# An eleven-stage encoder layer: the stage ends without GpSimd's drain and with one barrier instead of two; the merge's stores waited for one stage later

## The reference, cut to what matters

```python
u = _rmsnorm(h, g_mix); proj = u @ w_in                      # split into q, k, v, z, xbc, dt
att = _diff_attention(q, k, v, ...); ssm = _ssm_branch(z, xbc, dt, ...)
g_a, g_s = jnp.split(jax.nn.sigmoid(u @ w_gate + b_gate), 2, axis=-1)
merged = g_a * (att @ w_att_up) + g_s * (ssm @ w_ssm_up)
h = h + merged @ w_out
u2 = _rmsnorm(h, g_ffn)
h = h + _expert_choice(u2, w_router, w_exp_gate, w_exp_up, w_exp_down)   # 16 experts
ple_gate = jax.nn.sigmoid(h @ w_ple_gate + b_ple_gate)
h = h + ple_gate * (p @ w_ple_proj)
return _rmsnorm(h, g_final)
```

## Time and profile before

| what | value |
|---|---|
| median of 3 runs | 3064.95 us (3060.66 to 3067.93) |
| span of the profiled execution, first to last instruction | 3063.1 us |
| the profiled execution's own time | not listed apart from its span; the median is 1.9 us above the span |
| mean granted TensorE clock | 0.942 |
| busy share: TensorE, VectorE, ScalarE, GpSimd | 89%, 51%, 42%, 10% |
| DMA | 530.38 MB, mean 173 GB/s |

### The profile page before, as it was taken

How to read it: one execution, slowest core, us unless ns; L and a number is a source line. 1 busy time by engine, 2 the same in 40 slices (tenths; PEclk the granted TensorE clock), 3 DMA queues, 4 the chain that set the end, 5 groups by cost and what they waited for, 6 DMA issues and landing times. The chain is left out here.

```text
span 3063.1 us, 41071 instructions
## 1 busy us (share of the span) xinstructions
PE 2725.8 (89%) x15360; PEld 2333.1 (76%) x15360; DVE 1575.4 (51%) x2141; ACT 1291.4 (42%) x1801; POOL 313.8 (10%) x323
## 2 busy tenths in 40 slices
PE   6999999896788688596997987799999999999698
PEld 4899888685666266484885875699999999999686
DVE  5000000261776888312763227577777777777555
ACT  4111111141666754322542113355555555555445
POOL 1000000000000022211110002001101101101022
PEclk9999999898999899797998997699999999999899
DMA  5713112275320443846874644578878878878442
GB/s 181 228 69 104 69 69 77 87 243 155 79 79 22 126 134 106 264 157 219 281 257 151 205 137 167 169 230 246 262 231 246 259 234 247 259 234 246 150 156 90
DMA packets 422970, 530.38 MB, mean 173 GB/s; under 512 B 18424, under 2 KB 358280, under 8 KB 420840
## 3 DMA queue, kind: packets, MB, share of 16 engines
q1 hardware_dynamic: 391088, 396.13, 41.1%
q0 software_dynamic: 31776, 132.83, 13.4%
HBM read 400.78 MB, written 128.12 MB: 173 GB/s over the span
## 5 line engine op out<-in xcount | busy, mean ns | idle before, releaser
L2146 DVE TENSOR_TENSOR ex_w_lo<-ex_w_raw,ex_w_hi 128x2048 fp32r<-128x2048 f32 x195 | 443.9, 2291 | 142.8 <-ACT ex_w_hi L2103 142.8
L2235 PE MATMUL ex_ps_u<-ex_x,ex_w_hi 128*128 128x384 f32 x2048 | 411.6, 342 | 5.1 <-DVE ex_w_lo L2146 5.1
L2103 ACT ACTIVATE ex_w_hi<-ex_w_raw 128x2048 fp32r<-128x2048 f32 x195 | 370.5, 1909 | 0.8
L2235 PEld LDWEIGHTS ex_ps_u<-ex_x,ex_w_hi 128*128 128x128 f32 x2048 | 349.2, 189 | 6.2 <-issue 5.5
L2235 PEld LDWEIGHTS ex_ps_u<-ex_x,ex_w_lo 128*128 128x128 f32 x2048 | 265.7, 191 | 0.6
L2254 PE MATMUL ex_ps_d<-ex_w_hi,ex_h 128*128 128x512 f32 x768 | 266.0, 401 | 0.0
L2235 PE MATMUL ex_ps_u<-ex_x,ex_w_lo 128*128 128x192 f32 x2048 | 265.4, 273 | 0.0
L356 DVE TENSOR_TENSOR w_lo<-w_raw,w_hi 128x2048 fp32r<-128x2048 f32 x14 | 32.1, 2293 | 404.8 <-ACT w_hi L322 404.8
L328 ACT ACTIVATE stage<-ps 128x512 f32<-128x512 f32 (+1 forms) x102 | 55.7, 547 | 401.6 <-PE ps L380 336.7
L2254 PE MATMUL ex_ps_d<-ex_w_lo,ex_h 128*128 128x512 f32 x512 | 202.9, 396 | 0.0
L2254 PEld LDWEIGHTS ex_ps_d<-ex_w_hi,ex_h 128*128 128x128 f32 x768 | 144.7, 188 | 35.0
(11 more groups left out here) (393 smaller groups left out, 4933.0 us busy)
## 6 DMA issues: line engine op xcount, KB each, us to landing
ex_w_raw<-in_w_exp_gate SPq DMA_DIRECT2D x64, 1024.0 KB, 8.3
ex_w_raw<-in_w_exp_up SPq DMA_DIRECT2D x64, 1024.0 KB, 6.2
ex_w_raw<-in_w_exp_down SPq DMA_DIRECT2D x64, 1024.0 KB, 6.5
w_raw<-in_w_in SPq DMA_DIRECT2D x15, 1024.0 KB, 6.3
mg_w_raw<-in_w_ssm_up SPq DMA_DIRECT2D x24, 512.0 KB, 6.0
mg_g_raw<-g_d SPq DMA_DIRECT2D x24, 512.0 KB, 7.5
xbcT_d<-stage POOLq DMA_DIRECT2D x5, 1536.0 KB, 5.7
cv_raw<-xbcT_d POOLq DMA_DIRECT2D x10, 768.0 KB, 6.4
```

The source lines that it names most:

```text
L2103: act.activation(unit(w_hi, j), w_raw[:, j % RAW], ACT.Copy).then_inc(w_hi_done, 1)
L2146: dve.tensor_tensor(unit(w_lo, j), w_raw[:, j % RAW], unit(w_hi, j).bitcast(F32), ALU.subtract).then_inc(w_split, 1)
L2235: last = pe.matmul(ps_u[:, j % 2, m, 0:wide * C], w[:, s // 2, k, s % 2, cols], x[:, k, 0:wide].rearrange("p a c -> p (a c)"), start=i == ...
```

## The change

`Block()` gets `no_gpsimd_drain=True` in all eleven stages: the other four engines still drain, GpSimd does not, and all meet in one barrier of semaphores. The callback no longer clears and meets; it puts the stage's semaphores on a list, and the next stage's `open_block` has GpSimd clear that list at its start, while the other engines go on. After the last stage the list is cleared and one full `nc.all_engine_barrier()` follows, with a DRAIN on every engine, GpSimd's too. The semaphores of the merge's stores now live in `encoder_layer`; GpSimd no longer waits for the last stores at the end of `merge_branches`, SP does so in `project_out` before its loop that reads them. And SP's two increments of `m_in` come before its first loads.

```diff
@@ stage_semaphores
-    def clear():
-        nc.clear_and_free_semaphores(used)
-        nc.all_engine_barrier()
-    ctx.callback(clear)
+    ctx.callback(lambda: DONE_WITH.extend(used))
     return sem
+def open_block(nc, ctx):
+    if DONE_WITH:
+        nc.clear_and_free_semaphores(DONE_WITH)
+        DONE_WITH.clear()
+    return ctx.enter_context(nc.Block(no_gpsimd_drain=True))
@@ every stage
-        block = ctx.enter_context(nc.Block())
+        block = open_block(nc, ctx)
@@ merge_branches (its out_done is now the argument out_done)
-        out_done = [sem("out0"), sem("out1")]
...
-            for done in out_done:
-                pool.wait_ge(done, 32 * NU // 2)
             pool.wait_ge(next_in, 16 * 4)
@@ project_out, SP
             w_view = w_out.rearrange("(k p) (c n) -> c p k n", p=P, n=BLK)
+            for s in range(2):
+                sp.sem_inc(m_in[s], 32)
             for c, ks in enumerate(PARTS):
                 sp.dma_start(w_raw[:, ks], w_view[1, :, ks]).then_inc(w_in[c], 16)
...
             for s in range(2):
-                sp.sem_inc(m_in[s], 32)
                 sp.dma_start(xt[:, s], x[s]).then_inc(x_in[s], 16)
+            for done in m_stored:
+                sp.wait_ge(done, 32 * KT * NB // 2)
             with sp.Fori(0, TT // 2 - 1) as it:
@@ encoder_layer
+        m_stored = [nc.alloc_semaphore("m_stored%d" % s) for s in range(2)]
...
+        DONE_WITH.extend(m_stored)
...
             embed_and_norm(nc, tiles(h), tiles(ple), wg_hi, wg_lo0, w_ple_gate, b_ple_gate, g_final, ident, y_tiles)
+    nc.clear_and_free_semaphores(DONE_WITH)
+    DONE_WITH.clear()
+    nc.all_engine_barrier()
```

More of the change, by code:

```diff
@@ L43 @@
 START = 1
+DONE_WITH = []
 class Chain:
@@ L1442, in _, with merge_branches @@
                 sp.wait_ge(g_out[s], 16 * (NG // 2))
-def merge_branches(nc, g_d, o_hi_d, o_lo_d, yT_d, var_d, g_ssm_norm, w_att_up, w_ssm_up, b_gate, m_hi_d, m_lo_d, o_hi, o_lo, y_hi, y_lo, y_raw, w_out):
+def merge_branches(nc, g_d, o_hi_d, o_lo_d, yT_d, var_d, g_ssm_norm, w_att_up, w_ssm_up, b_gate, m_hi_d, m_lo_d, o_hi, o_lo, y_hi, y_lo, y_raw, w_out, out_done):
     KO = VW // P
@@ L1661, in _, with project_out @@
                 last.then_inc(full, 1)
-def project_out(nc, m_hi_d, m_lo_d, x, w_out, w_raw, m_slots, w_hi, w_lo, g_ffn, w_router, ident, logits, h_d, u2_d):
+def project_out(nc, m_hi_d, m_lo_d, x, w_out, w_raw, m_slots, w_hi, w_lo, g_ffn, w_router, ident, logits, h_d, u2_d, m_stored):
     HB = D // BLK
@@ L2482, in encoder_layer @@
             half_raw = keep("half_raw", [P, KT, BLK], F32)
-            merge_branches(nc, g, o_hi, o_lo, yT, var, g_ssm_norm, w_att_up, w_ssm_up, b_gate, m_hi, m_lo, *turned, *halves, half_raw, w_out)
-            project_out(nc, m_hi, m_lo, x, w_out, half_raw, turned[1], *halves, g_ffn, w_router, ident, logits, tiles(h), tiles(u2))
+            merge_branches(nc, g, o_hi, o_lo, yT, var, g_ssm_norm, w_att_up, w_ssm_up, b_gate, m_hi, m_lo, *turned, *halves, half_raw, w_out, m_stored)
+            project_out(nc, m_hi, m_lo, x, w_out, half_raw, turned[1], *halves, g_ffn, w_router, ident, logits, tiles(h), tiles(u2), m_stored)
+        DONE_WITH.extend(m_stored)
         with nc.sbuf_tensor("wg_hi", [P, KT, D], F32R) as wg_hi, nc.sbuf_tensor("wg_lo0", [P, KT, BLK], F32R) as wg_lo0:
```

## The result

| | before | changed |
|---|---|---|
| median of 4 runs each | 3063.44 us | 3045.79 us |
| range | 3060.66 to 3067.93 | 3041.91 to 3048.51 |
| ratio (95% interval) | | 0.9941 (0.9927 to 0.9955) |
| span of the profiled execution | 3063.1 us | 3046.9 us |

The change makes the kernel 17.7 us faster by the medians, 0.6%. The median of before, with one more run, is now 3063.44.

A forecast was written before the change was run, and what follows sets the result against it. TensorE, busy 2725.8 of 3063.1 us, bounds the kernel untouched; only time around the eleven stage ends can go. 7.8 + 4.4 + 7.0 + 1.9 = 21.1 us gained, 8.7 paid, 12.4 net: 3052.5 us, range 3042 to 3063.

The forecast's parts named there:

- The likeliest case: Whole kernel: 21.1 us gained, 8.7 paid at the last drain, 12.4 us faster, 3052.5 us; chance 0.42.
- the debt is forgotten: Rival: the clear or its short drain empties GpSimd's DMA list at no cost; 3043.8 us, chance 0.25.
- Part 1: Ends of `project`, `attend`, `run_experts`, where GpSimd drains last: the drains go, 7.8 us gained; the merge's is counted in part 3.
- Part 2: Ten stage ends: the second barrier goes, 5.7 us, less 0.8 for two GpSimd-led stages and 0.5 for the new barrier: 4.4 us.
- lists cleared in several pieces: Clears at stage openings: lists cleared in pieces add 0.1 to 0.3 us on GpSimd alone.
- Parts 3 and 4: Seam of merge and `project_out`: barrier 7.0 us earlier without GpSimd's drain, 1.9 us from `m_in` first; no stall at the opening.
- part 4: Start of `project_out`: `m_in` ahead of SP's loads lets TensorE start 1.0 us behind the barrier, gaining 1.9 us.
- Part 5: `project_out`: SP's moved wait for the merge's stores costs nothing; without its cover at most 2 us.
- Part 6: Program end: the last barrier's plain GpSimd drain walks 106 entries at 0.082 us, costing 8.7 us; bounds 0 and 21.0.
- The rule by the Trainium skill: GpSimd drains: a drain behind landed DMAs takes no time; the prediction rejected it on the merge's 4.70 us drain.

The follow-up runs named there:

- e1: The kernel before with only the blocks' GpSimd drain left away, clear and second barrier kept: 3050.82 against 3062.97 us.
- e3: The changed kernel with the blocks' GpSimd drain put back: 3053.40 us against 3062.97 for the kernel before.
- e8: The changed kernel without clears at the openings of `turn_attention` and the merge, lists cleared one opening later: 3040.79 us against 3062.64 for the kernel before.
- e10: The changed kernel with the `m_in` increments back behind SP's loads, run beside the changed kernel: 3044.90 us against its 3045.44.
- e2: The kernel before without the blocks' GpSimd drain, with a full barrier on either side of each clear: 3074.32 against 3062.97 us.
- e6: The changed kernel with no clear at the last stage's opening and a full barrier ahead of the last clear: 3050.29 us; changed kernel 3045.79.
- e5: The changed kernel with the two `m_in` increments back behind SP's loads: 3045.62 us; changed kernel 3045.79.
- e4: The kernel before with only the merge's stores waited for in `project_out` and `m_in` first; ends, clears, second barriers kept: 3058.42 against 3062.97 us.
- e9: The changed kernel once more, unedited: 3045.44 us against 3062.20 for the kernel before.
- e7: The changed kernel with no clear from the opening of `project_out` on and a full barrier ahead of the last clear: 3055.09 us; changed kernel 3045.79.

## Why the prediction was right, and where it was wrong

The time lay in the range and the sign held. The likeliest case was the wrong one: 12.4 us were forecast and 17.7 came. It is the rival "the debt is forgotten", given 0.25, that happened; 21.1 us of gain were its sum, and 17.7 and 16.8 its measurement. That the time fell between the two sums is partly luck: 3 to 4 us that no part had counted went at the merge's opening and to the clock.

**Part 1, right.** The drains that were last are worth 12.2 us alone (e1), against 12.5 by the earlier trace rows.

**Part 2, half right.** At all ten openings SP's first DMA comes 0.4 to 0.6 us sooner behind the last arrival at the barrier, as in `attend`, where it is 0.3 us (from SP's drain at 736.0 to 736.30) instead of 0.8 (736.95 to 737.78). What failed is the charge for the two stages whose first work hangs on GpSimd, `turn_attention` and the merge: 0.2 us of gain each was forecast. The price of "lists cleared in several pieces" was put at 0.1 to 0.3 us, but it is 0.6 at the merge's opening and 1.2 at `turn_attention`'s. The merge's first activation comes 2.0 us later against SP's first load than before (10.27 against 8.22, the latter from 1406.92 to 1415.14 in before's timeline). e3, which has the drains but the same clears, shows the same 10.48, so it is the clears; e8 takes it away. Counted from the last drain at the end of `turn_attention` (SP's, at 1406.7 and 1406.1) the first activation comes 10.6 us later instead of 9.0, a loss of 1.5 us where 0.2 of gain was forecast.

**Parts 3 and 4, right in the trace.** The seam's gap fell by 10.1 us, from 15.40 to 5.32; forecast 9.4 plus nothing for the first products. No stall came at the opening. The prediction's 12.1 us for 48 products are those of 40, since the row at 1661.88 in the earlier trace rows holds the last eight of them and the opening's first eight; the opening had some 1.8 us more room than it counted. TensorE's own start took 0.8 us behind the barrier, not 1.0. In time, however, part 4 is not resolved: e10 lost only 0.6 us in the stage.

**Part 5, right.** The moved wait costs nothing: SP issues its five loads and two of x back to back, and its reloads start at 1660.17, right behind TensorE's tile, as before. (Seven DMAs stand ahead of the wait, not nine; the last is issued by 1647.8, and the stores had landed at 1643.0.)

**Part 6, wrong.** "No plain drain has run since the launch" was true, and that a plain drain walks 82 ns an entry was true (e2, e6). The step that failed is that the last drain would find the list, the 8.7 us of the sum. It took 58 ns: the clears had emptied the list at every opening, and their short drains took 53 to 95 ns, apart from 213 in one of `turn_attention`'s and the 407 at the seam. The prediction had noticed that this drain takes longer than L77's and left it at 0.25. Read more closely, the rows of before could not decide it, since a plain drain always stood ahead.

**The rule by the Trainium skill** ("DMA: Bandwidth & Descriptors", "Anatomy of one DMA — SWDGE (gpsimd) path": the fixed cost of a DMA lies ahead of its semaphore) led to about the right time for the wrong reason. A drain behind landed DMAs does cost: 5.46 us in e6, 163 us after the last landing.

**The 3 to 4 us that are missing from 21.1.** 1.7 are the merge's opening (1.5 lost and 0.2 not gained). Some of the rest went to the clock, which the prediction took as neutral. At the same products of `convolve`, first before and then changed:

```profile
604.92 2.32 PE L596 MATMUL cv_ps_g<-u_hi,gw_hi 128*128 128x512 f32 x8
```

```profile
602.77 3.50 PE L602 MATMUL cv_ps_g<-u_hi,gw_hi 128*128 128x512 f32 x8
```

The view of the granted clock in the stretches around them (columns: stretch, length, PE busy, clock, DMA share, GB/s), before and changed:

```profile
603.00:608.00 5.00, 5.00 (x21) 0.84 0.01 3
1043.00:1053.00 10.00, 7.55 (x30) 0.90 0.45 134
```

```profile
600.70:605.70 5.00, 5.00 (x14) 0.54 0.00 0
1042.60:1052.60 10.00, 6.35 (x22) 0.83 0.50 147
```

In `convolve` the low stretch that follows the small transposes lasted 3.4 us before and 6.8 us in the changed kernel, and cost it 1.4 us; `scan_ssm` lost 1.7. Both stages' instructions are the same. In `scan_ssm` the profiles fall in two groups: without the walks at the ends ahead of it (changed, e1, e5 to e10) it takes 221.6 to 222.0 us, with them (before, e2, e3, e4) 220.3. That this goes with where the stage falls in time is argued from the rows, not tested. In `convolve` e9, e5 and e7 lost less than 1 us. On the other side, the low stretch at the seam shrank from 17.1 to 6.8 us.

## What to carry to other kernels

Ask of a GpSimd drain how many DMAs GpSimd has issued since the last clear: here it costs 82 ns for each, however long ago they landed, and it waits for those that are still in flight. So it takes the place of any wait that is moved away ahead of it (e4). A clear of semaphores emptied that list with a short drain of at most 0.5 us in every run, so a block end without the drain, followed by a clear at the next opening or one later (e8), pays nothing; a plain barrier ahead of the clear pays all (e2). Clears on GpSimd are free only where GpSimd's first DMA is not what the stage starts with. Clearing one stage later took the delay away in e8's trace; a clear behind GpSimd's first loads was not tried.

## What the runs showed that was not expected

The short drain in a clear neither walks the list nor waits for landings: at the seam it took 0.4 us with two stores in flight, and the last plain drain found nothing. A plain drain with DMAs in flight took 5.2 us at the merge (e3) and 7.2 at `convolve` (before). The list seems to have a limit that is not a number of DMAs: at 82 ns each, 66 of 66 were walked for the experts, 104 over the last stages' 155 (e7), but only 57 of 65 for the merge, whose transfers include the largest. For the merge alone a lower price per entry would give the same 4.7 us.

A load issued 0.6 us later, behind another queue's weights, was used 2.0 us later (10.27 against 8.23 us). And TensorE starting 2.4 us earlier at a seam won 0.6 us (e9 against e10), because the clock's low stretch of 6.8 us ran from 4.4 us behind the last product, and an earlier start put more products into it.
